# Query-key scores of the sliding-window layer: fp32 products or three float32r products of high and low parts

## The chip, the cores and the metric

One core of a Trainium2 chip runs one program. The metric is device time in microseconds; the kernel before takes 1897.34 us, the median of 3 runs (1896.95 to 1898.87).

## What is computed

A model of three blocks on 512 tokens of width 1024: gated linear attention with an MLP, sliding-window attention with an MLP, and a block with a convolution, dilated attention and a gated MLP. The change touches the attention of the second block. There 16 query heads of width 64 share 2 key heads, in blocks of 128 queries with a band of up to 256 keys:

```python
proj = h @ w_in + b_in
q, k, v = jnp.split(proj, [1024, 1152], axis=-1)
s = jnp.einsum('bnqkgd,bnskd->bnkgqs', q, kb).astype(jnp.float32) * (SWA_HEAD_DIM ** -0.5)
s = jnp.where(valid[None, :, None, None], s, -jnp.inf)
mx = jnp.maximum(jnp.max(s, axis=-1, keepdims=True), sink)
e = jnp.exp(s - mx)
p = e / (jnp.sum(e, axis=-1, keepdims=True) + jnp.exp(sink - mx))
o = jnp.einsum('bnkgqs,bnskd->bnqkgd', p.astype(vb.dtype), vb)
return o.reshape(B, T, 1024) @ w_out + b_out
```

## The kernel before, in words

Each engine has its own program, and the order of the work on an engine is the order in which its function is written. The engines meet through named events: `k.mark` raises one, `k.on` waits for it.

All large matrix products are made in parts. ScalarE rounds a weight tile to float32r (its high part, L1354), VectorE subtracts that from the tile (its low part, L2117), and TensorE adds three float32r products in a PSUM bank: high by high, low by high and high by low (`product`, L553 to L555). A product of an input-projection tile is 8 chunks of these three, 24 matmuls of 128x512.

The sliding-window layer (`t_swa`, `a_swa`, `v_swa`) works on the 8 pairs of heads p = 0 to 7, of which each pair takes one tile of 128 projected query columns: head s of the pair lies on partitions 64s to 64s+63, and both keys lie so in `WK`. The unit `u` is the key tile, `u+1` the value tile, and `u+2+p` the query tile of pair p. The tiles `u` to `u+3` are projected before the loop, in `t_starts`; `u+4` is projected at p = 0, `u+5` at p = 1, and so on to `u+9` at p = 5, all of these in PSUM bank 0. ScalarE brings each finished query tile from PSUM to `WQ`, scaled by 1/8 and with its bias (`evac`, L1674), and marks it with the event `ae`. That event does two things: `score(p)` on TensorE waits for it, and the next product in bank 0 waits for it, since the bank is then free.

In one turn of TensorE's loop stand, from p = 2 on: `score(p)`, `out(p-2)` (probabilities by values, L1112), the first half of the product of `u+4+p`, the transposes of head 2p-2 (L1098), the second half, and the transposes of head 2p-1. At p = 0 the first half of a product stands ahead of the score, and at p = 1 there is no `out` between the score and the product. At p = 6 and 7 pieces of the output projection (`ahead`, L584 to L586) stand where the products were.

`score(p)` is 8 fp32 matmuls of half rows (L1083): four query blocks by two heads, of 128 keys for the first block and 256 for the others. The two heads of a block follow each other and use different rows and different banks. The trace shows each fp32 matmul as two instructions, so 16 for each score.

In one turn of VectorE's loop stand: the masked row maxima of heads 2p and 2p+1 (`score`, L2665), the low part of an attention output (`low`, L2694), the low part of a weight tile (`v_cut`, L2117), the division of head 2p (`weigh`, L2677 to L2683), a copy of transposed probabilities (`turn`, L2690) and the division of head 2p+1. ScalarE has the exponentials (`expo`, L1694, L1696), the query evacuation, the copies of transposed probabilities (L1686) and the high part of the attention output (`high`, L1701):

```python
    for p in range(8):
        score(2 * p)
        score(2 * p + 1)
        if p >= 2:
            low(p - 2)
        v_cut(e, k, u + min(p, 6) + 7)
        weigh(2 * p)
        if p >= 1:
            turn(2 * p - 1)
        weigh(2 * p + 1)
```

Of the kernel before, what the change touches and what calls it, by code (L numbers as in the profile page):

```python
# [8 lines left out]
F32 = mybir.dt.float32  # L9
# [4 lines left out]
T = 512  # L14
# [9 lines left out]
KB = 1024  # L24
# [236 lines left out]
def memory(nc):  # L261
# [77 lines left out]
    m.SVH = over("SVH", [128, 4, 4, 256], rows, F32R)  # L339

    m.WQ = arena("WQ", [128, 8, T], 0)
    m.PW = arena("PW", [128, 4, 896], 16)
    m.PTW = arena("PTW", [128, 2, 896], 30)
    m.WOH = arena("WOH", [128, 8, T], 37, F32R)
# [714 lines left out]
def t_swa(e, k):  # L1059
    m, ps = k.m, k.m.ps  # L1060
    u = k.at["swa_in"]

    def set_v():
        e.wait_ge(*k.on("ae", u + 1))
        e.wait_ge(*k.on(*k.free[7]))
        for t in range(4):
            x = e.transpose(ps[7][:, t * 128:(t + 1) * 128], m.WQ[:, 7, t * 128:(t + 1) * 128], cst(m, "ident"))
        x.then_inc(*k.mark("wvt"))
        k.free[7] = ("wv",)

    def score(p):

        e.wait_ge(*k.on("ae", u + 2 + p))
        e.wait_ge(*k.on("ae", u))
        for g, group in enumerate(SWA_GROUPS):
            f = 0
            for s in range(2):
                e.wait_ge(*k.on(*k.free[SWA_BANKS[g][s]]))
            for blk in group:
                k0, n = SWA_KEYS[blk]  # L1080
                for s in range(2):
                    b, half = SWA_BANKS[g][s], slice(64 * s, 64 * s + 64)
                    x = e.matmul(ps[b][:, f:f + n], m.WQ[half, p, blk * 128:(blk + 1) * 128], m.WK[half, k0:k0 + n],  # L1083
                                 start=True, stop=True)
                    if blk == group[-1]:
                        x.then_inc(*k.mark("score", "w", 2 * p + s, g))
                        k.free[b] = ("smax", "w", 2 * p + s, g)
                f += n

    def turn(i):  # L1090

        for g in range(2):
            b, f = (3, 6)[g], 0
            e.wait_ge(*k.on("pn", "w", i))
            e.wait_ge(*k.on(*k.free[b]))
            for j, blk in SWA_TURNS[g]:
                c = SWA_PLACE[blk] + j * 128 - SWA_KEYS[blk][0]
                x = e.transpose(ps[b][:, f:f + 128], m.PW[:, i % 4, c:c + 128], cst(m, "ident"))  # L1098
                f += 128
            x.then_inc(*k.mark("turn", "w", i, g))  # L1100
            k.free[b] = ("ptv" if i % 2 and g else "pta", "w", i, g)

    def out(p):

        e.wait_ge(*k.on("wv"))
        e.wait_ge(*k.on(*k.free[7]))
        for j, f in ((0, 0), (2, 256), (1, 512), (3, 768)):
            n = min(256, 512 - 128 * j)
            for s in range(2):
                i, half = 2 * p + s, slice(64 * s, 64 * s + 64)  # L1110
                e.wait_ge(*k.on("ptv" if s and j % 2 else "pta", "w", i, j % 2))
                x = e.matmul(ps[7][half, 128 * j:128 * j + n], m.WV[:, j, half], m.PTW[:, s, f:f + n], start=j == 0,  # L1112
                             stop=j == 3, skip_group_check=True)
                if j == 3:
                    x.then_inc(*k.mark("pv", "w", i))
        k.free[7] = ("wol", p)

    t_starts(e, k, u, "mix1", ["ae"] * 4)
    set_v()
    def ahead(c, n, f):  # L1120

        w = k.at["swa_out"]
        tokens(e, k, w + c, n, m.WOH, m.WOL, c, 0, 0, None, lambda c: [("wol", c)], c == 0, False, (f,))

    for p in range(8):
        if p:
            score(p)
        if p >= 2:
            out(p - 2)
        if p < 6:  # L1130
            product(e, k, u + 4 + p, m.HH, m.HL, 2, 0, ev="ae", c1=4)
            if p == 0:
                score(p)
            if p >= 1:
                turn(2 * p - 2)
            product(e, k, u + 4 + p, m.HH, m.HL, 2, 0, ev="ae", c0=4)
            if p >= 1:
                turn(2 * p - 1)
        else:
            if p == 6:  # L1140
                ahead(0, 2, 0)
            turn(2 * p - 2)
            if p == 6:
                ahead(2, 1, 0)
            else:
                ahead(3, 1, 0)
                ahead(0, 2, 1)
            turn(2 * p - 1)
            if p == 7:
                ahead(2, 2, 1)  # L1150

    def between(n):
        if n == 0:
            out(6)
        elif n < 3:
            turn(13 + n)
        else:
            out(7)

    t_ends_early(e, k, k.at["swa_out"], m.WOH, m.WOL, "mlp1", "mv", lambda c: [("wol", c)], between)  # L1160
# [494 lines left out]
def a_swa(e, k):  # L1655
    m, ps = k.m, k.m.ps
    u = k.at["swa_in"]
    bq8 = m.SMALL[:, 56:64]
    e.wait_ge(*k.on("par"))
    e.activation(bq8, par(m, "swa_bq"), AF.Copy, scale=0.125).then_inc(*k.mark("b8", 0))  # L1660
    e.activation(m.SMALL[:, 55:56], par(m, "qn"), AF.Copy, scale=0.125).then_inc(*k.mark("b8", 1))

    def evac(j):
        p = psum(k, u + j)
        e.wait_ge(*k.on("unit", u + j))
        if j == 0:
            e.activation(m.WK[:, :], p, AF.Identity, bias=par(m, "swa_bk")).then_inc(*k.mark("ae", u + j))
        elif j == 1:
            e.activation(m.WQ[:, 7, :], p, AF.Identity, bias=par(m, "swa_bv")).then_inc(*k.mark("ae", u + j))
        else:  # L1670
            e.wait_ge(*k.on("b8", 0))
            if j == 9:
                e.wait_ge(*k.on("wvt"))
            e.activation(m.WQ[:, j - 2, :], p, AF.Identity, bias=bq8[:, j - 2:j - 1], scale=0.125).then_inc(  # L1674
                *k.mark("ae", u + j))

    def set_v():
        e.wait_ge(*k.on("wvt"))
        e.activation(m.WV[:, :, :], ps[7][:, :].rearrange("p (t f) -> p t f", t=4), AF.Copy).then_inc(*k.mark("wv"))

    def turn(i, g):
        a, b = SWA_COLS[g]
        e.wait_ge(*k.on("turn", "w", i, g))
        if i >= 2:
            e.wait_ge(*k.on("pv", "w", i - 2))
        e.activation(m.PTW[:, i % 2, a:b], ps[(3, 6)[g]][:, 0:b - a], AF.Copy).then_inc(*k.mark("pta", "w", i, g))  # L1686

    def expo(i):
        st = m.STAT[:, i % 4, :]
        nm, sm = st[:, 4:8], st[:, 8:12]  # L1690
        e.wait_ge(*k.on("nmax", "w", i))
        for blk in range(4):
            p = m.PW[:, i % 4, SWA_PLACE[blk]:SWA_PLACE[blk] + SWA_KEYS[blk][1]]
            e.activation(p, p, AF.Exp, bias=nm[:, blk:blk + 1], accum_out=sm[:, blk:blk + 1]).then_inc(  # L1694
                *k.mark("exp", "w", i, blk))
        e.activation(st[:, 12:16], nm, AF.Exp, bias=par(m, "sinks", 8 * (i % 2) + i // 2, 1)).then_inc(  # L1696
            *k.mark("exp", "w", i, 4))

    def high(c):
        e.wait_ge(*k.on("pv", "w", 2 * c + 1))  # L1700
        e.activation(m.WOH[:, c, :], ps[7][:, :], AF.Copy).then_inc(*k.mark("woh", c))  # L1701

    for j in range(1, 5):
        a_cut(e, k, u + j + 3)
        evac(j - 1)
    set_v()
    for p in range(8):
        a_cut(e, k, u + min(p, 6) + 7)
        if p == 1:
            turn(0, 0)  # L1710
            turn(0, 1)
        if p < 7:
            expo(2 * p)
        if p >= 2:
            if p != 6:
                high(p - 2)
            turn(2 * p - 2, 0)
            turn(2 * p - 2, 1)
            if p == 6:
                high(p - 2)  # L1720
        if p == 7:
            expo(2 * p)
            turn(2 * p - 1, 0)
        if p == 0:
            evac(p + 4)
        expo(2 * p + 1)
        if 0 < p < 6:
            evac(p + 4)
        if 1 <= p < 7:
            turn(2 * p - 1, 0)  # L1730
    high(6)
    turn(14, 0)
    turn(14, 1)
    turn(15, 0)
    high(7)
    a_ends(e, k, k.at["swa_out"], k.at["up10"], "post_mix1", "mlp1", early=True)
# [914 lines left out]
def v_swa(e, k):  # L2651
# [40 lines left out]
    def low(c):  # L2692
        e.wait_ge(*k.on("woh", c))
        e.tensor_tensor(m.WOL[:, c, :], ps[7][:, :], m.WOH[:, c, :].bitcast(F32), A.subtract).then_inc(*k.mark("wol", c))  # L2694

    for j in range(1, 5):
        v_cut(e, k, u + j + 3)
    for p in range(8):
        score(2 * p)
        score(2 * p + 1)  # L2700
# [4 lines that stand above are left out]
        if p >= 1:  # L2705
            turn(2 * p - 1)
        weigh(2 * p + 1)
    low(6)
    turn(15)
    low(7)  # L2710
# [730 lines left out]
```

## Time and profile before

| what | value |
|---|---|
| median of the runs | 1897.34 us |
| the profiled execution's own time | 1897.22 us |
| its span | 1895.4 us |
| TensorE busy | 1888.0 us of the span |
| VectorE busy | 1344.2 us |
| ScalarE busy | 987.4 us |
| granted TensorE clock | 1.000 |
| sliding-window attention | about 586 to 675 us of the span |

The span runs from the first to the last instruction; the own time of the execution is 1.8 us longer. Shares are means over stages: a wait of TensorE counts fully only where TensorE is the engine that everything else keeps up with.

### The profile page before, as it was taken

The page shows a single profiled execution, that of the slowest core. Times are in us where ns is not written, and L with a number is a line of the kernel's source. Part 1 is how long each engine was busy: PE and PEld are TensorE (multiplying, and loading weights), DVE is VectorE, ACT ScalarE, POOL GpSimd, SP SyncE. Part 2 cuts the span into 40 slices and gives each one's busy share as a digit, 9 for nine tenths or more (in the row PEclk, how much of TensorE's full clock was granted, in tenths as well). Part 3 has the DMA queues.
Part 4 walks back from the last instruction along what each step waited for, and adds up shares of the span by engine and source line. Part 5 has one row for each costly group of instructions (what it writes and reads, how often), then busy time and mean ns, then how long its engine had stood idle before and what let it go on. Part 6 is the DMA issues. An engine that isn't in the chain of part 4 may idle for free. (4 is left out here: it accounts for less than half of the span.)

```text
span 1895.4 us, 25267 instructions
## 1 busy us (share of the span) xinstructions
PE 1888.0 (100%) x9396; PEld 1551.5 (82%) x9396; DVE 1344.2 (71%) x2000; ACT 987.4 (52%) x1591; POOL 96.0 (5%) x114
## 2 busy tenths in 40 slices
PE   9999999999999999999999999999999999999999
PEld 8877888888888788888888888667788888888887
DVE  8656665656566766665666788998897876767867
ACT  5634464444546756454544335788435455545454
POOL 0100000101000000000100000000000000100101
PEclk9999999999999999999999999999999999999999
DMA  6632156757323114756641346232224634644735
GB/s 227 161 100 101 67 152 174 167 164 207 126 69 143 46 66 132 192 145 178 173 160 67 122 134 171 85 95 73 90 95 139 167 93 153 156 150 117 199 96 123
DMA packets 70684, 249.79 MB, mean 132 GB/s; under 512 B 7970, under 2 KB 8226, under 8 KB 69924
## 3 DMA queue, kind: packets, MB, share of 16 engines
q1 hardware_dynamic: 56448, 198.82, 30.4%
q0 software_dynamic: 13824, 49.29, 14.7%
q8 instruction: 77, 1.26, 0.3%
q14 instruction: 43, 0.35, 0.1%
q10 hardware_dynamic: 292, 0.07, 0.0%
HBM read 246.05 MB, written 2.10 MB: 131 GB/s over the span
## 5 line engine op out<-in xcount | busy, mean ns | idle before, releaser
L553 PE MATMUL ps<-HH,WH 128*128 128x512 f32 (+1 forms) x1664 | 620.5, 373 | 0.0
L555 PE MATMUL ps<-HH,WL 128*128 128x512 f32 (+1 forms) x1664 | 615.5, 370 | 0.0
L554 PE MATMUL ps<-HL,WH 128*128 128x512 f32 (+1 forms) x1664 | 615.4, 370 | 0.0
L1354 ACT ACTIVATE WH<-WR 128x1024 fp32r<-128x1024 f32 x331 | 346.8, 1056 | 474.9 <-PE ps L555 311.2
L2117 DVE TENSOR_TENSOR WL<-WR,WH 128x1024 fp32r<-128x1024 f32 x330 | 400.7, 1219 | 262.4 <-ACT WH L1354 262.0
L553 PEld LDWEIGHTS ps<-HH,WH 128*128 128x128 f32 x1664 | 313.5, 188 | 62.8 <-issue 10.0
L555 PEld LDWEIGHTS ps<-HH,WL 128*128 128x128 f32 x1664 | 313.5, 188 | 53.7
L554 PEld LDWEIGHTS ps<-HL,WH 128*128 128x128 f32 x1664 | 313.7, 189 | 52.0
L1012 PE MATMUL ps<-WH,AH 128*128 128x512 f32 x490 | 190.6, 389 | 0.0
L1013 PE MATMUL ps<-WH,AL 128*128 128x512 f32 x490 | 190.6, 389 | 0.0
L1014 PE MATMUL ps<-WL,AH 128*128 128x512 f32 x490 | 190.6, 389 | 0.0
L2726 DVE SCALAR_TENSOR_TENSOR M<-AP,PAR,M 128x512 f32<-128x512 f32 x240 | 167.1, 757 | 0.1
L1013 PEld LDWEIGHTS ps<-WH,AL 128*128 128x128 f32 x490 | 92.0, 188 | 19.2
L1012 PEld LDWEIGHTS ps<-WH,AH 128*128 128x128 f32 x490 | 92.0, 188 | 19.1
L1014 PEld LDWEIGHTS ps<-WL,AH 128*128 128x128 f32 x490 | 92.0, 188 | 19.1
L2006 ACT ACTIVATE UP<-ps 128x512 f32<-128x512 f32 x44 | 26.3, 598 | 117.6 <-PE ps L555 117.6
L3179 POOL DMA_DIRECT2D WR<-in_quart x48 | 41.8, 988 | 813.5 <-DMA WR<-in_quart 745.8
L3040 DVE SCALAR_TENSOR_TENSOR RW<-UP,PAR,RW 128x512 f32<-128x512 f32 x44 | 33.1, 752 | 44.0 <-ACT RW L2012 43.3
L3040 DVE SCALAR_TENSOR_TENSOR M<-UP,PAR,M 128x512 f32<-128x512 f32 x44 | 33.1, 752 | 38.0 <-ACT M L2012 37.3
L1611 ACT ACTIVATE RW<-RW 128x512 f32<-128x512 f32 x64 | 40.5, 632 | 2.0
L1808 ACT ACTIVATE P<-P,SMALL 128x128 f32<-128x128 f32 (+1 forms) x64 | 35.1, 550 | 11.2 <-DVE SMALL L2761 11.2
L1363 ACT ACTIVATE HL<-X 128x1024 fp32r<-128x1024 f32 x22 | 23.3, 1059 | 33.0 <-DVE X L2178 24.7
(401 smaller groups left out, 2614.5 us busy)
## 6 DMA issues: line engine op xcount, KB each, us to landing
WR<-in_up SPq DMA_DIRECT2D x96, 512.0 KB, 4.3
WR<-in_quart SPq DMA_DIRECT2D x60, 512.0 KB, 3.5
WR<-in_quart POOLq DMA_DIRECT2D x48, 512.0 KB, 6.1
WR<-in_in SPq DMA_DIRECT2D x48, 512.0 KB, 3.5
WR<-in_down SPq DMA_DIRECT2D x16, 512.0 KB, 3.4
WR<-in_quartf SPq DMA_DIRECT2D x14, 512.0 KB, 3.5
WR<-in_quartf POOLq DMA_DIRECT2D x14, 512.0 KB, 5.5
MT<-in_up SPq DMA_DIRECT2D x12, 512.0 KB, 3.6
```

What stands on the lines that cost most here:

```text
L553: e.matmul(ps, wh, hi[:, c, cols], start=c == 0 and not (shared and h), stop=False, skip_group_check=shared)
L554: e.matmul(ps, wh, lo[:, c, cols], start=False, stop=False, skip_group_check=shared)
L555: y = e.matmul(ps, wl, hi[:, c, cols], start=False, stop=c == x.n - 1, skip_group_check=shared)
L1012: e.matmul(m.ps[b + v], xh, x.wh[:, w], start=start and q == 0, stop=False, skip_group_check=last)
L1013: e.matmul(m.ps[b + v], xl, x.wh[:, w], start=False, stop=False, skip_group_check=last)
L1014: y = e.matmul(m.ps[b + v], xh, x.wl[:, w], start=False, stop=stop and q == n - 1, skip_group_check=last)
L1354: e.activation(x.wh[:, 0:n], raw(m, x.raw)[:, 0:n], AF.Copy).then_inc(*k.mark("whi", u))
L1611: e.activation(buf, buf, AF.Square).then_inc(*k.mark("sqr", u))
L2117: e.tensor_tensor(x.wl[:, 0:n], raw(m, x.raw)[:, 0:n], x.wh[:, 0:n].bitcast(F32), A.subtract).then_inc(*k.mark("wlo", u))
L2726: e.scalar_tensor_tensor(m.M[:, c, :], m.AP[:, c, t:t + T], par(m, "conv_w", c * 31 + t, 1), m.M[:, c, :], A.mult, A.add).then_inc(*k.mark ...
L3040: e.scalar_tensor_tensor(tmp, m.UP[:, 2 * (i % 2) + g, t:t + T], par(m, "fcw", (i + FC2 * g) * 3 + t, 1), tmp, A.mult, A.add).then_inc(*k. ...
L3179: e.dma_start(raw(m, x.raw)[:, 0:128 * x.n], x.more, accum_op=A.add).then_inc(*k.mark(f"added{x.raw}", u + j, by=16))
```

## The change

The scores are made from parts too. The scale of 1/8 and the key bias go into the key tile `WK`, of which ScalarE makes the high part `WKH` and VectorE the low part `WKL`. ScalarE now writes a query tile from PSUM, with its bias, straight to its high part `WQH`, which has two buffers. A new instruction of VectorE, `low_q(p)`, reads the same PSUM bank, adds the bias, subtracts `WQH` and writes the low part `WQL`; it marks `hlo`. Both `score(p)` and the next product in bank 0 now wait for `hlo` in place of `ae`. Each score is 24 float32r matmuls in place of 8 fp32 ones. `low_q(0)` and `low_q(1)` stand among the weight cuts ahead of VectorE's loop, `low_q(p+2)` is the last thing of turn p, for p = 0 to 5.

```diff
@@ t_swa
     def score(p):
-        e.wait_ge(*k.on("ae", u + 2 + p))
-        e.wait_ge(*k.on("ae", u))
+        e.wait_ge(*k.on("hlo", u + 2 + p))
+        e.wait_ge(*k.on("hlo", "k"))
+        qh, ql = m.WQH[:, p % 2, :], m.WQL[:, p, :]
...
-                for s in range(2):
-                    b, half = SWA_BANKS[g][s], slice(64 * s, 64 * s + 64)
-                    x = e.matmul(ps[b][:, f:f + n], m.WQ[half, p, blk * 128:(blk + 1) * 128], m.WK[half, k0:k0 + n],
-                                 start=True, stop=True)
+                for j, (query, key) in enumerate(((qh, m.WKH), (qh, m.WKL), (ql, m.WKH))):
+                    for s in range(2):
+                        b, half = SWA_BANKS[g][s], slice(64 * s, 64 * s + 64)
+                        x = e.matmul(ps[b][:, f:f + n], query[half, blk * 128:(blk + 1) * 128], key[half, k0:k0 + n],
+                                     start=j == 0, stop=j == 2)
...
-    t_starts(e, k, u, "mix1", ["ae"] * 4)
+    t_starts(e, k, u, "mix1", ["ae", "ae", "hlo", "hlo"])
...
-            product(e, k, u + 4 + p, m.HH, m.HL, 2, 0, ev="ae", c1=4)
+            product(e, k, u + 4 + p, m.HH, m.HL, 2, 0, ev="hlo", c1=4)
...
-            product(e, k, u + 4 + p, m.HH, m.HL, 2, 0, ev="ae", c0=4)
+            product(e, k, u + 4 + p, m.HH, m.HL, 2, 0, ev="hlo", c0=4)
@@ a_swa, evac(j)
         if j == 0:
-            e.activation(m.WK[:, :], p, AF.Identity, bias=par(m, "swa_bk")).then_inc(*k.mark("ae", u + j))
+            e.wait_ge(*k.on("b8", 0))
+            e.activation(m.WK[:, :], p, AF.Identity, bias=bk8, scale=0.125).then_inc(*k.mark("ae", u + j))
+            e.wait_ge(*k.on("ae", u + j))
+            e.activation(m.WKH[:, :], m.WK[:, :], AF.Copy).then_inc(*k.mark("hhi", "k"))
...
-            e.activation(m.WQ[:, j - 2, :], p, AF.Identity, bias=bq8[:, j - 2:j - 1], scale=0.125).then_inc(
-                *k.mark("ae", u + j))
+            if j > 3:
+                e.wait_ge(*k.on("score", "w", 2 * j - 7, 1))
+            e.activation(m.WQH[:, j % 2, :], p, AF.Identity, bias=par(m, "swa_bq", j - 2, 1)).then_inc(*k.mark("ae", u + j))
@@ v_swa
+    def low_q(p):
+        e.wait_ge(*k.on("ae", u + 2 + p))
+        if p == 7:
+            e.wait_ge(*k.on("wvt"))
+        e.scalar_tensor_tensor(m.WQL[:, p, :], psum(k, u + 2 + p), par(m, "swa_bq", p, 1), m.WQH[:, p % 2, :].bitcast(F32),
+                               A.add, A.subtract).then_inc(*k.mark("hlo", u + 2 + p))
+
     for j in range(1, 5):
         v_cut(e, k, u + j + 3)
+        if j == 1:
+            e.wait_ge(*k.on("hhi", "k"))
+            e.tensor_tensor(m.WKL[:, :], m.WK[:, :], m.WKH[:, :].bitcast(F32), A.subtract).then_inc(*k.mark("hlo", "k"))
+        elif j > 2:
+            low_q(j - 3)
...
         weigh(2 * p + 1)
+        if p < 6:
+            low_q(p + 2)
```

TensorE at p = 1, before: the score of the second pair and the start of the next product. `s_ae` is the event of ScalarE's evacuation.

```order
L1083 MATMUL ps<-WK,WQ 128x128 [waits s_smax,s_ae]
L1083 MATMUL ps<-WK,WQ 128x128
L1083 MATMUL ps<-WK,WQ 128x256 x2
L1083 MATMUL ps<-WK,WQ 128x256 [waits s_smax]
L1083 MATMUL ps<-WK,WQ 128x256 x3
L553 MATMUL ps<-HH,WH 128x512 [waits s_ae,s_wlo]
L554 MATMUL ps<-HL,WH 128x512
```

The same place after the change:

```order
L1089 MATMUL ps<-WKH,WQH 128x128 [waits s_smax,s_hlo]
L1089 MATMUL ps<-WKH,WQH 128x128
L1089 MATMUL ps<-WKL,WQH 128x128 x2
L1089 MATMUL ps<-WKH,WQL 128x128 x2
L1089 MATMUL ps<-WKH,WQH 128x256 x2
L1089 MATMUL ps<-WKL,WQH 128x256 x2
L1089 MATMUL ps<-WKH,WQL 128x256 x2
L1089 MATMUL ps<-WKH,WQH 128x256 [waits s_smax]
...
L557 MATMUL ps<-HH,WH 128x512 [waits s_hlo,s_wlo]
```

The score has 24 matmuls in place of 8, and both it and the product behind it wait for VectorE's `s_hlo`.

VectorE at the end of turn p = 0, before: the division of head 1 (`s_exp` is ScalarE's last exponential of a head), then the maxima of head 2.

```order
L2677 TENSOR_TENSOR SMALL<-SMALL 128x4 [waits s_exp]
L2679 RECIPROCAL SMALL<-SMALL 128x4 [waits s_sum]
L2683 TENSOR_SCALAR PW<-PW,SMALL 128x128 [waits s_den]
L2683 TENSOR_SCALAR PW<-PW,SMALL 128x256 [waits s_den] x3
L2665 ISA PW,SMALL<-ps,CONST 128x128 [waits s_par,s_score]
```

The same place after the change:

```order
L2684 TENSOR_TENSOR SMALL<-SMALL 128x4 [waits s_exp]
L2686 RECIPROCAL SMALL<-SMALL 128x4 [waits s_sum]
L2690 TENSOR_SCALAR PW<-PW,SMALL 128x128 [waits s_den]
L2690 TENSOR_SCALAR PW<-PW,SMALL 128x256 [waits s_den] x3
L2707 SCALAR_TENSOR_TENSOR WQL<-ps,PAR,WQH 128x512 [waits s_ae]
L2672 ISA PW,SMALL<-ps,CONST 128x128 [waits s_par,s_score]
```

The low part of the third query tile stands behind the division of head 1, and ahead of the maxima of head 2.

## Rows read from the trace of the kernel before

**Rows 1.** The page, span, busy time and granted clock.

```profile
span 1895.4 us, 25267 instructions
...
PE 1888.0 (100%) x9396; PEld 1551.5 (82%) x9396; DVE 1344.2 (71%) x2000; ACT 987.4 (52%) x1591; POOL 96.0 (5%) x114
...
PEclk9999999999999999999999999999999999999999
```

**Rows 2.** Waits of PE: us in total, times, longest us.

```profile
PE ps L941 <- DVE SMALL L3141: 1.2, 1, 1.2
```

**Rows 3.** Timeline, PE at p = 1: start us, us, engine, line, operation [idle before].

```profile
590.90 1.79 PE L1083 MATMUL ps<-WK,WQ 64*128 64x128 f32 x16
592.62 0.50 PE L553 MATMUL ps<-HH,WH 128*128 128x512 f32 x1
```

**Rows 4.** Timeline, ACT and DVE between 588 and 596 us.

```profile
588.04 0.43 DVE L2665 CUSTOM_DVE_ANT_0 PW<-ps,CONST 128x256 f32<-128x256 f32 x1 [0.22 <-PE ps L1083]
...
591.19 0.67 ACT L1674 ACTIVATE WQ<-ps,SMALL 128x512 f32<-128x512 f32 x1
...
593.62 0.29 ACT L1696 ACTIVATE SMALL<-SMALL,PAR 128x4 f32<-128x4 f32 x1
...
...
595.34 0.28 DVE L2665 CUSTOM_DVE_ANT_0 PW<-ps,CONST 128x128 f32<-128x128 f32 x1
```

**Rows 5.** Groups by line and form: count, busy us, mean ns of one.

```profile
L2319 DVE SCALAR_TENSOR_TENSOR LA<-ps,LA 128x512 f32<-128x512 f32 x4 | 2.5, 684 | 2.1 <-ACT LA L1471 2.1
L2743 DVE SCALAR_TENSOR_TENSOR QK<-QK,PAR,AT 128x512 f32<-128x512 f32 x8 | 6.0, 745 | 0.0
```

**Rows 6.** Timeline: one pair of score instructions, and whole-row float32r matmuls of 256 columns.

```profile
592.31 0.38 PE L1083 MATMUL ps<-WK,WQ 64*128 64x256 f32 x2
...
568.57 0.28 PE L554 MATMUL ps<-HL,WH 128*128 128x256 f32 x1
568.69 0.28 PE L555 MATMUL ps<-HH,WL 128*128 128x256 f32 x1
```

**Rows 7.** Timeline, PE and its weight loads (PEld) around `out(0)`, p = 2.

```profile
601.61 2.42 PE L1112 MATMUL ps<-PTW,WV 128*64 128x256 f32 x16
...
602.30 1.49 PEld L1112 LDWEIGHTS ps<-PTW,WV 128*64 128x64 f32 x14 [0.50 <-ACT PTW L1686]
```

**Rows 8.** Timeline, one whole turn, p = 3, from 611 us.

```profile
611.29 0.56 DVE L2690 COPY PTW<-ps 128x384 f32<-128x384 f32 x1 [1.04 <-PE ps L1098]
...
613.15 0.28 DVE L2665 CUSTOM_DVE_ANT_0 PW<-ps,CONST 128x128 f32<-128x128 f32 x1
...
614.56 0.50 PE L553 MATMUL ps<-HH,WH 128*128 128x512 f32 x1
...
618.07 0.98 ACT L1686 ACTIVATE PTW<-ps 128x512 f32<-128x512 f32 x2 [0.65 <-PE ps L1098]
```

**Rows 9.** Timeline, DVE and ACT, from the end of p = 5 to p = 7.

```profile
643.21 0.56 DVE L2690 COPY PTW<-ps 128x384 f32<-128x384 f32 x1 [1.25 <-PE ps L1098]
...
645.07 0.28 DVE L2665 CUSTOM_DVE_ANT_0 PW<-ps,CONST 128x128 f32<-128x128 f32 x1
...
646.70 0.40 ACT L1694 ACTIVATE PW<-PW,SMALL 128x128 f32<-128x128 f32 x1 [2.14 <-DVE SMALL L2671]
...
650.22 0.69 DVE L2694 TENSOR_TENSOR WOL<-ps,WOH 128x512 fp32r<-128x512 f32 x1 [2.05 <-ACT WOH L1701]
650.83 1.22 DVE L2117 TENSOR_TENSOR WL<-WR,WH 128x1024 fp32r<-128x1024 f32 x1
...
653.36 0.55 DVE L2690 COPY PTW<-ps 128x384 f32<-128x384 f32 x1
```

**Rows 10.** Timeline, PE: `out(4)`, `out(5)` and `out(6)`.

```profile
644.82 1.73 PE L1112 MATMUL ps<-PTW,WV 128*64 128x256 f32 x16
...
652.09 2.74 PE L1112 MATMUL ps<-PTW,WV 128*64 128x256 f32 x16
...
659.88 2.02 PE L1112 MATMUL ps<-PTW,WV 128*64 128x256 f32 x16
```

More of the change, by code:

```diff
@@ L341, in memory @@
     m.WQ = arena("WQ", [128, 8, T], 0)
+    m.WQL = arena("WQL", [128, 8, T], 0, F32R)
+    m.WKL = over("WKL", [128, T], acc, F32R)
+    m.WKH = over("WKH", [128, T], dg + 2 * KB, F32R)
+    m.WQH = over("WQH", [128, 2, T], tmp, F32R)
     m.PW = arena("PW", [128, 4, 896], 16)
@@ L1080, in score @@
                 k0, n = SWA_KEYS[blk]
-                for s in range(2):
-                    b, half = SWA_BANKS[g][s], slice(64 * s, 64 * s + 64)
-                    x = e.matmul(ps[b][:, f:f + n], m.WQ[half, p, blk * 128:(blk + 1) * 128], m.WK[half, k0:k0 + n],
-                                 start=True, stop=True)
-                    if blk == group[-1]:
-                        x.then_inc(*k.mark("score", "w", 2 * p + s, g))
-                        k.free[b] = ("smax", "w", 2 * p + s, g)
+                for j, (query, key) in enumerate(((qh, m.WKH), (qh, m.WKL), (ql, m.WKH))):
[3 more added lines that the diff above has]
+                                     start=j == 0, stop=j == 2)
+                        if blk == group[-1] and j == 2:
+                            x.then_inc(*k.mark("score", "w", 2 * p + s, g))
+                            k.free[b] = ("smax", "w", 2 * p + s, g)
                 f += n
@@ L1657, in a_swa @@
     u = k.at["swa_in"]
-    bq8 = m.SMALL[:, 56:64]
+    bk8 = m.SMALL[:, 56:57]
     e.wait_ge(*k.on("par"))
-    e.activation(bq8, par(m, "swa_bq"), AF.Copy, scale=0.125).then_inc(*k.mark("b8", 0))
+    e.activation(bk8, par(m, "swa_bk"), AF.Copy, scale=0.125).then_inc(*k.mark("b8", 0))
     e.activation(m.SMALL[:, 55:56], par(m, "qn"), AF.Copy, scale=0.125).then_inc(*k.mark("b8", 1))
@@ L1670, in evac @@
         else:
-            e.wait_ge(*k.on("b8", 0))
-            if j == 9:
-                e.wait_ge(*k.on("wvt"))
-            e.activation(m.WQ[:, j - 2, :], p, AF.Identity, bias=bq8[:, j - 2:j - 1], scale=0.125).then_inc(
-                *k.mark("ae", u + j))
+            if j > 3:
+                e.wait_ge(*k.on("score", "w", 2 * j - 7, 1))
+            e.activation(m.WQH[:, j % 2, :], p, AF.Identity, bias=par(m, "swa_bq", j - 2, 1)).then_inc(*k.mark("ae", u + j))
     def set_v():
```

## Prediction

> **What bounds the kernel now.** I read the page first. TensorE is busy for 1888.0 us of a span of 1895.4 us, at the full granted clock (2.4 GHz) throughout [rows 1], and the waits of TensorE name none longer than 1.2 us [rows 2]. So the kernel is bound by what TensorE has to do, and a change counts in two ways only: by how much shorter its instructions get, and by waits that it puts into a row of instructions that has none. The other engines have time to spare, VectorE 551 us, but only where nobody waits for the place at which their new work stands. After the page I read the timeline of the attention turn by turn, for that.
>
> **The scores themselves.** One score starts at 590.90 and the next product at 592.62: 1.72 us [rows 3]. It is 16 instructions of 0.38 us each; they fit because the two heads start together, on different rows [rows 6]. So a score is 8 pairs, six of 256 columns and two of 128. An fp32 instruction takes each column twice: six pairs of 512 cycles and two of 256 are 3584 cycles, at 2.4 GHz 1.49 us; the other 0.23 us are the start and the change to the next kind of matmul.
>
> After the change a score is 12 pairs of float32r: nine of 256 columns, three of 128. The trace has no float32r matmul on half rows. The nearest row is the float32r matmul on whole rows with 256 columns: they follow each other by 0.12 us [rows 6]. If a pair costs what one whole-row matmul costs, and 128 columns no less than 256 (a load of weights stands ahead of each either way), a score takes 12 x 0.12 + 0.23 = 1.67 us, which **saves 0.05 us**. The bounds: if the pairs run at the bare stream rate, (9 x 256 + 3 x 128) / 2.4 GHz = 1.12 us, plus 0.23, the score saves 0.37 us; if the two heads do not overlap, 24 x 0.12 + 0.23 = 3.11 us, it costs 1.39 us more. I take 0.05, the value of the nearest row with the overlap that the fp32 pairs show.
>
> **The new wait at p = 1.** This is the main term. The product of `u+5` stands right behind `score(1)` and goes into bank 0. Before, the bank was free once ScalarE had evacuated `u+4`, from 591.19 to 591.86 [rows 4], so the product started at 592.62 without waiting. Now it must wait for `low_q(2)`, and that stands on VectorE behind both divisions of turn 0. The division of head 1 waits for the last exponential of head 1, which ends at 593.91; the next thing on VectorE started at 595.34 [rows 4]. That is where `low_q(2)` starts, less the 0.05 us by which `score(0)` is shorter: the second group of maxima did wait for that score [rows 4], and everything behind hangs on it. So it starts at 595.29. The price of `low_q` is that of a scalar_tensor_tensor of 128x512 from PSUM, 0.684 us [rows 5]; the same from SBUF with a parameter column takes 0.745 us [rows 5], the upper bound. It ends at 595.97, and with 0.05 us to hand over (as from ScalarE's copy to the loads at 602.30 [rows 7], whose copy ended at 602.25) the product starts at 596.02. **The cost is 596.02 - 592.62 = 3.40 us**, and what both scores save is already inside it. Behind the product wait the transposes, `score(2)` and all the rest of TensorE's list. VectorE and ScalarE don't get ahead by it for long: ScalarE's copies and exponentials of turn 1 stand behind the transposes of head 0, which stand behind this product, so they move by the same 3.40 us.
>
> **p = 2.** `out(0)` started at 601.61 but had to wait for ScalarE's copy until 602.30 [rows 7]. That chain moves with the transposes and not with the score, so the score's gain is lost here: **0**. `low_q(3)` ends some 0.5 us before the product needs the bank.
>
> **p = 3, 4, 5.** In turn 3 VectorE's copy starts at 611.29, released by TensorE, and the division of head 5 is over when the maxima begin at 613.15; `low_q(4)` would then run from 613.15 to 613.84, and the product starts at 614.56 [rows 8]. So there are 0.7 us of slack and no wait. `low_q` pushes everything behind it on VectorE back by 0.61 us (an instruction of 0.69 us is followed after 0.61 [rows 9]): the maxima, through them the exponentials, the high part and the copy of ScalarE that starts at 618.07 with 0.65 us of idle time ahead of it [rows 8]. It just fits. VectorE too gets to its next copy with 1.04 us to spare [rows 8]. So each of these turns gains the score's 0.05: **-0.15 us**.
>
> **p = 6 and 7.** Here the cover is gone. From the copy at 643.21, released by TensorE's transposes of head 9, VectorE and ScalarE hand over to each other without TensorE: division, [`low_q(7)`], maxima of head 12, exponentials (ScalarE idle until 646.70), high part, low part at 650.22, weight cut, division, and the copy at 653.36 [rows 9], for which `out(5)` waits: it takes 2.74 us in place of the 1.73 of `out(4)`, which waits for nothing [rows 10]. `low_q(7)` stands in this chain, so `out(5)` ends 0.61 us later, and the gains of scores 6 and 7 are lost in it. The same chain goes on to `out(6)`, which also waits (2.02 us [rows 10]); it is the same delay, not a second one. **+0.61 us**.
>
> **What costs nothing.** The extra copy of the keys on ScalarE, `WKL` and the first two `low_q` fall into time in which both engines wait for TensorE's first four products, 0.7 us each against idle times of several us. If `low_q(1)` were late it would hold the second half of `score(0)`; by the end of the weight cut ahead of it, it has about 0.7 us to spare. `low_q` and ScalarE's evacuation read the same bank one after the other.
>
> **Sum.** 3.40 + 0 - 0.15 + 0.61 = **+3.86 us**, on the profiled execution's own 1897.22 us; that execution lies 0.12 us under the median of 1897.34, so against the median I say 1901.2 us. What a measurement of this kernel can tell from no change is about 0.2%, 3.8 us: the sum falls right on this bound.
>
> **Rivals.** *The heads do not overlap* (each score +1.39 us). The wait at p = 1 grows to 3.40 + 0.05 + 1.39 = 4.84, since the chain hangs on `score(0)`; p = 2 hides 0.69 of it (+0.70); three turns 4.17; and at p = 6 the score ends at 644.82 [rows 10] + 1.39 while VectorE would be ready at 645.07 [rows 9] + 0.61: 0.53 on top of 0.61. Sum 10.85, 1908.2 us. For it: no such matmul is in the trace. Against: the fp32 pairs overlap, and with weight loads of the same width.
>
> *Loads don't overlap within a row group.* In this kernel a load for head 0 would then stand behind head 0's running matmul; a pair would take its 256 columns, 0.107 us, and then a load, at most 0.12 since a load and a matmul fit into that on whole rows [rows 6]: 12 x 0.227 + 0.23 = 2.95, +1.23 per score. By the same places: 4.68 + 0.54 + 3.69 + 0.98 = 9.89, 1907.2 us. Against it speak the whole-row matmuls, which reload the same rows each time and still follow by 0.12 [rows 6]. The Trainium skill (TensorE: Matmul & The Clock Gate, "The mechanism") says that weight loads overlap running matmuls only when the row group differs; by that rule this rival would be the forecast. The trace does not agree: 0.12 us for 256 columns leaves no room for a load of its own.
>
> *The clock falls in the wait.* TensorE stands still for about 3.4 us at p = 1, far longer than any wait of the trace before [rows 2], in which the clock never fell [rows 1]. If it fell to 1.2 GHz for the 12 matmuls behind the wait, which take 2.8 us, they would take 2.8 us more: 1904.0 us. The Trainium skill (TensorE: Matmul & The Clock Gate, "Part 1: The HAM clock gate") says the clock is halved after an idle stretch; no row of before can show it.
>
> *The wait is given back*, the case on the other side. TensorE waits later for `out(0)` 0.69, `out(5)` 1.01 and `out(6)` 0.29 us; if the engines behind got ahead during the 3.40 us, these 1.99 us would vanish, the 0.61 with them, and scores at the bare stream rate would save 0.37 in five turns, 1.85: 3.40 - 1.99 - 1.85 = -0.44, 1896.9 us. It decides from a gain of 3.4 us on. Against: the chains to these waits begin at transposes that stand behind the wait.
>
> **Chances.** The forecast 0.68, of which a little over half lies over the bound (0.36 slower, 0.32 same, as scores at the stream rate would bring it down by 1.0); no overlap 0.04 and loads apart 0.04, slower; the clock 0.12, slower; given back 0.07, same; the rest 0.05, 0.03 faster and 0.02 same. That makes faster 0.03, same 0.41, slower 0.56. The range from 1899.3 to 1905.5 holds the forecast with its bounds and the clock, 0.80: below, scores at the stream rate (five turns and the chain, 6 x 0.32 = 1.9), above, the clock with another 1.5 for score or VectorE prices at their upper ends.
>
> **What would show it.** In the profile after: one idle stretch of TensorE of 3.3 to 3.5 us ahead of the product at about 592.5 us, released by VectorE's `WQL`; scores of 24 matmuls in 1.6 to 1.7 us, begun in pairs; `out(5)` longer by 0.3 to 0.7 us; no other new wait. Scores of over 2 us, or no idle stretch at p = 1, would make it wrong.

## The result, and the profile after

The changed kernel takes **1902.85 us** (median of 8 runs, 1902.32 to 1904.29), against 1897.32 us for the kernel before (8 runs, measured together with it): a ratio of 1.003, 95% interval 1.0021 to 1.0039. It is 5.5 us slower. The profiled execution is the first of the runs, 1902.32 us. Its page, the lines that answer to [rows 1]:

```profile
span 1900.5 us, 25405 instructions
...
PE 1888.4 (99%) x9460; PEld 1553.6 (82%) x9460; DVE 1350.2 (71%) x2009; ACT 988.7 (52%) x1592; POOL 96.2 (5%) x114
...
PEclk9999999999999999999999999999999999999999
```

The span is 5.1 us longer, while TensorE's busy time is only 0.4 us longer. So most of it is idle time of TensorE. A slower clock does not show as idle time, and shorter scores can hide it in the sum of the busy time, so it has to be looked for by itself. The waits of PE (us in total, times, longest) name the first; it answers to [rows 2]:

```profile
PE ps L557 <- DVE WQL L2707: 3.7, 1, 3.7
PE ps L945 <- DVE SMALL L3162: 1.2, 1, 1.2
PE ps L1104 <- ACT PTW L1693: 0.6, 1, 0.6
```

There is one wait of 3.7 us, of the product (L557, was L553) for the low part of a query tile. The second row was there before; the third is new. The timeline at p = 1, where [rows 3] and [rows 4] were read (start us, us, engine, line, operation, in brackets the idle time before):

```profile
590.34 0.33 PE L1089 MATMUL ps<-WKH,WQH 64*128 64x128 f32 x2
...
590.65 0.67 ACT L1682 ACTIVATE WQH<-ps,PAR 128x512 fp32r<-128x512 f32 x1
...
593.81 1.07 DVE L2690 TENSOR_SCALAR PW<-PW,SMALL 128x128 f32<-128x128 f32 x4
594.79 0.75 DVE L2707 SCALAR_TENSOR_TENSOR WQL<-ps,PAR,WQH 128x512 fp32r<-128x512 f32 x1
...
595.69 0.47 PE L557 MATMUL ps<-HH,WH 128*128 128x512 f32 x1 [3.67 <-DVE WQL L2707]
```

The tile was ready for `low_q(2)` at 591.32, when ScalarE's evacuation ended. It ran at 594.79, behind both divisions, for 0.75 us; the product started 0.15 us later. The next stretch is what the page does not show, since its 40 slices are too coarse: the windows of TensorE (stretch, length, busy time with the number of instructions, granted clock with 1.00 for 2.4 GHz, DMA share, GB/s).

```profile
593.00:595.50 2.50, 0.00 (x0) 1.00 0.00 0
595.50:596.70 1.20, 1.01 (x4) 0.96 0.00 0
596.90:600.10 3.20, 3.20 (x10) 0.51 0.00 0
600.20:603.60 3.40, 3.40 (x20) 1.00 0.47 159
```

After the wait the clock is full for the first matmuls, then half (1.2 GHz) for 8 of them, then full again. The timeline there:

```profile
595.99 0.40 PE L558 MATMUL ps<-HL,WH 128*128 128x512 f32 x1
596.23 0.39 PE L559 MATMUL ps<-HH,WL 128*128 128x512 f32 x1
...
598.02 0.63 PE L558 MATMUL ps<-HL,WH 128*128 128x512 f32 x1
598.45 0.63 PE L559 MATMUL ps<-HH,WL 128*128 128x512 f32 x1
```

They follow each other by 0.23 to 0.24 us first (0.30 behind the very first), and by 0.43 in the slow stretch. These are busy times, so no list of waits holds them.

**Where the time went.** One place can be compared between all runs without the small differences elsewhere: from the start of `score(0)` to the first transposes of the next layer, on TensorE. Before, that is 586.22 to 693.57; after, 585.79 to 698.54:

```profile
693.57 0.60 PE L608 MATMUL ps<-CONST,MT 128*128 128x128 f32 x4
```

```profile
698.54 0.93 PE L612 MATMUL ps<-CONST,MT 128*128 128x128 f32 x7
```

| stretch on TensorE, us | before | after | difference |
|---|---|---|---|
| `score(0)` to the product of p = 1 | 6.40 | 9.89 | +3.49 |
| that product's start to the transposes of head 0 | 2.87 | 4.41 | +1.54 |
| on to `out(4)` at p = 6 | 49.32 | 48.91 | -0.41 |
| on to the end of the layer | 48.75 | 49.53 | +0.78 |
| together | 107.34 | 112.75 | +5.41 |

What lies outside this stretch took 1788.1 us before and 1787.8 after; over all profiled executions of this study it ranges from 1787.4 to 1789.1, and of that part the kernels change only a few instructions ahead of `score(0)`. So differences of under 1 us are read from the stretch, with the medians beside them.

### The profile page after: what moved, and what is told of

The parts are those of the page before. It is cut to its first block and busy times, and to the rows that moved or that the text cites. A ratio compares the mean times of both kernels' runs of the same rounds, so it can differ in the third digit from the quotient of the medians.

```text
span 1900.5 us, 25405 instructions
## 1 busy us (share of the span) xinstructions
PE 1888.4 (99%) x9460; PEld 1553.6 (82%) x9460; DVE 1350.2 (71%) x2009; ACT 988.7 (52%) x1592; POOL 96.2 (5%) x114
## 5 line engine op out<-in xcount | busy, mean ns | idle before, releaser
L557 PE MATMUL ps<-HH,WH 128*128 128x512 f32 (+1 forms) x1664 | 621.1, 373 | 3.7 <-DVE WQL L2707 3.7
L557 PEld LDWEIGHTS ps<-HH,WH 128*128 128x128 f32 x1664 | 313.8, 189 | 66.4 <-issue 13.2
```

What stands on the lines that cost most here:

```text
L557: e.matmul(ps, wh, hi[:, c, cols], start=c == 0 and not (shared and h), stop=False, skip_group_check=shared)
```

## The experiments

### The clock by itself

The first four kernels (`e1_fill` to `e4_fp32`) were measured together, and the kernel before took 1897.11 us there (27 runs). The first fills the wait with work:

```diff
+FILL = 14
...
+        if p == 1:
+            e.wait_ge(*k.on("wv"))
+            for _ in range(FILL):
+                x = e.matmul(ps[7][:, :], m.HH[:, 0, 0:128], m.HH[:, 1, :], start=True, stop=True)
+            x.then_inc(*k.mark("fill"))
+            k.free[7] = ("fill",)
```

> The changed kernel with 14 more float32r matmuls of 128x512 behind score(1), into PSUM bank 7, whose result nothing reads: they fill the wait for low_q(2), which itself stays. Theory (the time is the wait of 3.5 us, plus the clock at half rate behind it, 1.5 us): TensorE never stands still for long, the granted clock stays at 1.00, and the kernel takes 1.5 us less than the changed one, about 1901.3 us. Rival (the slow matmuls behind the wait have another cause, such as a refill after a wait or contention with VectorE): the matmuls behind the wait stay slow and the time stays at 1902.8, or more.

Measured: 1901.1 us (1900.6 to 1902.47, 11 runs), 1.75 under the changed kernel, or 1.54 when each is taken against its own kernel before (3.99 over 1897.11, 5.53 over 1897.32); the stretch is 111.17, 1.58 shorter. The timeline at p = 1 and two of the same windows:

```profile
591.91 3.47 PE L1138 MATMUL ps<-HH 128*128 128x512 f32 x14
595.66 0.47 PE L558 MATMUL ps<-HH,WH 128*128 128x512 f32 x1 [0.28 <-DVE WQL L2714]
```

```profile
595.50:596.70 1.20, 1.04 (x5) 1.00 0.00 0
596.90:600.10 3.20, 3.20 (x19) 1.00 0.02 5
```

The product starts at 595.66, as late as in the changed kernel, since it waits for the same instruction. But the clock stays at 1.00, and the 3.2 us that held 10 matmuls now hold 19. More work on TensorE made the kernel faster: the slow matmuls came from the idle stretch, and their price is the 1.54 us of the table.

### The wait by itself

The second gives the product of p = 0 another bank, so that the product of p = 1 does not have to wait for `low_q(2)`. The value transposes take bank 0 for it.

```diff
@@ t_swa
-            x = e.transpose(ps[7][:, t * 128:(t + 1) * 128], m.WQ[:, 7, t * 128:(t + 1) * 128], cst(m, "ident"))
+            x = e.transpose(ps[0][:, t * 128:(t + 1) * 128], m.WQ[:, 7, t * 128:(t + 1) * 128], cst(m, "ident"))
...
-        k.free[7] = ("wv",)
+        k.free[0] = ("wv",)
...
-            product(e, k, u + 4 + p, m.HH, m.HL, 2, 0, ev="hlo", c1=4)
+            product(e, k, u + 4 + p, m.HH, m.HL, 2, 0 if p else 7, ev="hlo", c1=4)
...
```

> The changed kernel with one thing moved: the value transposes use bank 0 in place of 7, and the product of p = 0 uses bank 7 in place of 0, so the product of p = 1 waits for an evacuation that is long over and not for low_q(2). All instructions of the change stay. Theory (bank 0 is what couples TensorE to the tail of VectorE's turn): no idle stretch at p = 1, no fall of the clock, scores of 1.6 us; left are the 0.7 us of p = 6 and 7 less 0.1 us for each score that is not hidden (five of them): 1897.3 plus 0.1, about 1897.4 us. Rival (VectorE is too full, and the wait comes back at p = 2 or at the scores): 1900 us or more.

Measured: 1898.0 us (1897.8 to 1898.37, 11 runs), ratio to before 1.0004 (0.9995 to 1.0013); the stretch is 108.28. Wait and fall of the clock are gone, and with them 4.47 us of the 5.41 in the stretch. But it is 0.6 us above the expectation, and the list of waits says where:

```profile
PE ps L1118 <- ACT PTW L1693: 1.1, 2, 1.0
PE ps L1104 <- ACT PTW L1693: 0.6, 1, 0.6
```

`out(0)` (L1118) now waits 1.0 us for ScalarE's copy. I come back to it with `e6_q2`.

### The scores by themselves

```diff
-        e.wait_ge(*k.on("hlo", u + 2 + p))
+        e.wait_ge(*k.on("ae", u + 2 + p))
-        qh, ql = m.WQH[:, p % 2, :], m.WQL[:, p, :]
+        qh, ql = m.WQH[:, p % 2, :], m.WQH[:, p % 2, :]
...
-        if p < 6:
-            low_q(p + 2)
```

> The changed kernel without any low_q: the low part of the queries is not computed, the third product of a score takes the high part again, so its row of 24 float32r matmuls stays; score and product wait for ScalarE's evacuation as before the change. Theory (float32r scores save 0.11 us each, but only where nothing else is waited for: p = 0, 1, 3, 4, 5; low_q costs everything else): 1897.3 - 0.55 = 1896.8 us, no wait at p = 1, and out(5) and out(6) end as before. Rival (the float32r scores cost in another place, or save in all eight turns): over 1897.3, or 1896.4.

Measured: 1896.63 us (1896.17 to 1897.33, 11 runs), ratio 0.9997 (0.9988 to 1.0006); the stretch is 106.96, 0.38 less than before. This kernel leaves out the low part of the queries, so its scores are less exact; only its time is of use. The direction and the mechanism agree. The size is somewhat under the expected 0.55, and the interval of the runs holds no change as well. From `out(4)` on it takes 48.91 us, against 48.75 before and 49.53 after the change: without any `low_q` most of the loss at the end is gone. That is the third term by subtraction, 0.6 us.

### The scores as before, with the wait

```diff
-                for j, (query, key) in enumerate(((qh, m.WKH), (qh, m.WKL), (ql, m.WKH))):
+                for j, (query, key) in enumerate(((q32, m.WK),)):
```

> The changed kernel with the scores as before: 8 fp32 matmuls each, on the unsplit keys (the low part of the keys is not made) and on the rounded queries; low_q and all waits for it stay, and its result is not used. Theory (wait, clock and the chain at p = 6 cost 5.7 us, the shorter scores give 0.4 back): 0.4 us slower than the changed kernel, about 1903.2 us, with the same idle stretch at p = 1, 0.1 longer. Rival (the scores' new form is what costs): near 1897.3.

Measured: 1904.08 us (1903.0 to 1905.53, 5 runs), ratio 1.0037 (1.0024 to 1.0049); the stretch is 113.02, 0.27 over the changed kernel. Its product of p = 1 starts 10.01 us behind `score(0)`, 0.12 more. The rival, that the new form of the scores costs, is out: with the old form the loss is as large. The medians differ by 1.2 us, three times the expected 0.4, and more than the stretch; 0.6 of it lies outside the stretch in the profiled execution, and with 5 runs the cause of that stays open.

The clock fell here too. The idle stretch ahead of the product is 3.54 us (596.40), the granted clock is 0.50 from there on, and from 596.96 the matmuls follow each other by 0.42 to 0.43 us up to 599.09, then by 0.23 again. From the product to the transposes of head 0 it takes 4.23 us, against 2.87 before the change and 4.41 after it. So the fall is seen behind two idle stretches of this length, at a price of 1.36 and 1.54 us.

### The place of one instruction

The kernels `e5_first` to `e8_q2q7r` were measured together (before: 1897.15 us, 33 runs), and `e9_mid` to `e11_best` likewise (before: 1897.33 us, 27 runs). `e5_first` leaves the banks of the change and moves `low_q(2)`:

```diff
         v_cut(e, k, u + min(p, 6) + 7)
+        if p == 0:
+            low_q(2)
         weigh(2 * p)
...
-        if p < 6:
+        if 0 < p < 6:
             low_q(p + 2)
```

> The changed kernel with low_q(2) moved on VectorE from behind both divisions of turn 0 to ahead of them; banks as in the change. Theory (the position of one instruction makes the wait, and a short wait leaves the clock alone): low_q(2) runs as soon as ScalarE's evacuation is over (591.9), the wait shrinks from 3.7 to about 0.7 us, the granted clock stays at 1.00, maxima and exponentials of turn 1 come no later: 1897.1 + 0.7 + 0.7 (chain at p = 6) - 0.55 = about 1898.0 us. Rival (any wait at this place drops the clock): 1899.5 or more.

Measured: 1897.55 us (1896.99 to 1898.6, 11 runs), ratio 1.0 (0.9992 to 1.0009); the stretch is 107.75, so 5.00 us of 5.41 are back. The wait is even shorter than expected:

```profile
591.58 0.75 DVE L2707 SCALAR_TENSOR_TENSOR WQL<-ps,PAR,WQH 128x512 fp32r<-128x512 f32 x1 [1.30 <-ACT WQH L1682]
...
592.47 0.47 PE L557 MATMUL ps<-HH,WH 128*128 128x512 f32 x1 [0.23 <-DVE WQL L2707]
```

VectorE had been idle for 1.30 us when `low_q(2)` could start. Between this kernel and the changed one lies the place of one instruction, and nearly the whole loss.

A wait between the two comes from the third possible place, behind the first division:

```diff
         weigh(2 * p)
+        if p == 0:
+            low_q(2)
...
-        if p < 6:
+        if 0 < p < 6:
             low_q(p + 2)
```

> The changed kernel with low_q(2) between the two divisions of turn 0. By the timeline of VectorE the first division ends at about 592.7, low_q(2) at 593.4: a wait of 1.5 us ahead of the product of p = 1, between the 0.2 of e5_first and the 3.7 of the change. Theory (a wait costs its length, and the clock falls only behind the long one): clock 1.00 throughout, 1.3 us more than e5_first, about 1898.8 us. Rival (the clock falls behind this one too): about 1900.3 us.

Measured: 1898.88 us (1898.06 to 1900.14, 11 runs), ratio 1.0008 (0.9999 to 1.0017). Its waits of PE and its cores:

```profile
PE ps L557 <- DVE WQL L2707: 1.0, 1, 1.0
```

```profile
core 0: 1897.1 us, clock 1.000
```

The clock stays full behind this wait. The stretch is 108.52, 0.77 over e5_first; I had expected 1.3. `low_q(2)` ended at 593.16 where I had put it at 593.4, and the score ended at 592.25 and not at 591.9. So a wait of 1.0 us costs its length alone, and only those of 3.5 and 3.7 us cost 1.4 to 1.5 more. No run has a wait between 1.0 and 3.5 us.

### The wait of `out(0)`

```diff
         score(2 * p)
+        if p in (1,):
+            low_q(p + 1)
         score(2 * p + 1)
...
-        if p < 6:
+        if 0 < p < 6:
             low_q(p + 2)
```

> The kernel with the swapped banks (e2_bank), low_q(2) moved once more: between the maxima of head 2 and head 3. In e2_bank out(0) waited 1.0 us for ScalarE's copy, 0.8 more than before: my theory is that low_q(2) ahead of the maxima delays the exponentials of head 2 and with them that copy. Then here out(0) waits as before the change and the kernel takes 0.7 us less than e2_bank, 1897.3. Rival (the copy is late because TensorE came 0.7 us earlier to it): no gain, 1898.0.

Measured: 1897.56 us (1897.17 to 1898.44, 11 runs), ratio 1.0001 (0.9993 to 1.001); the stretch is 107.87, 0.41 under e2_bank. First e2_bank, then this kernel: when VectorE finished the maxima of head 2 (L2678), and how `out(0)` went on behind ScalarE's copy.

```profile
596.77 0.23 DVE L2678 TENSOR_SCALAR SMALL<-SMALL,PAR 128x4 f32<-128x4 f32 x1
...
602.36 1.73 PE L1118 MATMUL ps<-PTW,WV 128*64 128x256 f32 x14 [0.97 <-ACT PTW L1693]
```

```profile
596.19 0.23 DVE L2678 TENSOR_SCALAR SMALL<-SMALL,PAR 128x4 f32<-128x4 f32 x1
...
601.88 1.73 PE L1118 MATMUL ps<-PTW,WV 128*64 128x256 f32 x14 [0.41 <-ACT PTW L1693]
```

Both explanations hold in part. Moved, `low_q(2)` no longer delays the maxima, and `out(0)` waits 0.41 in place of 0.97. What is left is that TensorE gets there earlier: counted from the start of `score(0)`, `out(0)` goes on with its weight loads behind the copy after 16.05 us here (601.88) and after 16.08 before the change (602.30 in [rows 7]), so the copy is as early as it was.

### The end of the layer

```diff
@@ e7_q2q7 against e6_q2: v_swa
         score(2 * p)
-        if p in (1,):
+        if p in (1, 6):
             low_q(p + 1)
...
-        if 0 < p < 6:
+        if 0 < p < 5:
             low_q(p + 2)
@@ e8_q2q7r: also t_swa, p = 6
-            if p == 6:
-                ahead(0, 2, 0)
             turn(2 * p - 2)
             if p == 6:
+                ahead(0, 2, 0)
                 ahead(2, 1, 0)
```

> As e6_q2, and low_q(7) too between the maxima of heads 12 and 13, so that it leaves the chain of p = 6 that ends in the wait of turn(11) and out(5); the pieces of the output projection at p = 6 then wait for it, about 0.8 us, where TensorE has about 1 us to spare before out(5). Theory: 0.4 to 0.7 us less than e6_q2, about 1896.8. Rival (the new wait is handed on whole): the same as e6_q2 or 0.2 more.

> As e7_q2q7, and on TensorE at p = 6 the transposes of head 10 stand ahead of the first piece of the output projection, so that nothing waits for low_q(7). Theory: the chain is as before the change and all of the scores' gains that are left outside waits stay, 1896.6, 0.5 under the kernel before. Rival: the transposes then wait for a bank, no better than e7_q2q7.

Measured: e7 1897.73 us (1897.24 to 1898.23, 11 runs), e8 1897.01 us (1896.3 to 1897.86, 11 runs); ratios 1.0001 (0.9993 to 1.001) and 0.9998 (0.9989 to 1.0007). The stretches are 108.08 and 107.24. From `out(4)` to the end it is 49.52 us in e6, 49.74 in e7, 48.88 in e8 and 48.75 before the change. My expectation of `e7_q2q7` fell, and its rival holds: the delay is handed on whole. In e7 the output projection's first piece (L588) is late by 1.0 us, the longest of these two waits:

```profile
PE ps L588 <- issue: 1.4, 2, 1.0
```

The list names no engine for it. But the piece uses bank 0, which `low_q(7)` frees, and that ended at 646.41, 0.07 us ahead of the weight load of this piece (646.48). This pushes back the transposes of head 10, and they are themselves a link of the chain to `out(5)`, through ScalarE's copy. e8 takes them out of the way, and then the end of the layer costs 0.13 us more than before the change in place of 0.78. So the chain is what I took it for, but it has a link on TensorE that I had left out. No run has the new order on TensorE without the move of `low_q(7)`, so how much of the 0.65 us the order alone would give, in this kernel or in the one before, stays open.

### How much room there is in the middle turns

```diff
         if 0 < p < 6:
             low_q(p + 2)
+            if p < 5:
+                e.wait_ge(*k.on("hlo", u + 4 + p))
+                low_q(p + 2)
```

> e5_first with low_q done twice in turns 1 to 4, the second behind the first: 0.8 us more on VectorE per turn, with no use. The prediction called low_q free in these turns, with 0.7 us of room ahead of the product and 0.65 us on ScalarE. Theory (it is free, and the room is nearly used up): each of four products now waits about 0.3 us, 1.2 us in all, about 1898.8 us. Rival (there is much more room): 1897.6 us as e5_first.

Measured: 1898.56 us (1898.23 to 1900.64, 11 runs), ratio to before 1.0008 (0.9999 to 1.0017); the stretch is 109.00, 1.25 over e5_first. All of it lies between the first transposes and `out(4)`: 50.22 us in place of 48.92.

```profile
PE ps L557 <- DVE WQL L2707: 1.5, 5, 0.3
```

Five products wait, for 0.3 us each at most. One of the five is that of p = 1, with the 0.2 of e5_first; the four others are those of the doubled instructions. One `low_q` per turn is hidden, a second is not: it adds 0.78 us to VectorE's turn, and 0.3 of that reaches TensorE. So there was room for about 0.5 us more, and not for 0.7. In the changed kernel `low_q(4)` ended at 618.51, 0.54 us ahead of the product at 619.05, and the hand-over takes 0.14 of that.

### Both moves together

`low_q(2)` ahead of the divisions as in e5_first, the end as in e8_q2q7r, the banks of the change.

> The two moves that paid, together, with the banks of the change: low_q(2) ahead of both divisions of turn 0 (e5_first), low_q(7) between the maxima of heads 12 and 13 and the transposes of head 10 ahead of the first piece of the output projection (e8_q2q7r). Theory (all that is left is 0.11 us for each score outside a wait): over the stretch from score(0) to the end of the layer 0.4 us less than before the change, 1896.8 us, which the runs can hardly tell from 1897.15. Rival (the two moves don't add, since the wait of out(0) is there in both): 1897.2 us.

Measured: 1896.75 us (1896.23 to 1898.01, 11 runs); ratio 0.9998 (0.9989 to 1.0007). The stretch is 107.09, 0.25 less than before the change. The moves add: 5.66 us against the changed kernel in the stretch, where the first gave 5.00 (`e5_first`) and the second 0.63 (`e8_q2q7r` against `e6_q2`). Against the kernel before no gain can be told from none.

## Why the prediction was right, and where it was off

The time of 1902.85 us lies in the range of 1899.3 to 1905.5, and it is slower, as the larger chance said. The forecast of 1901.2 was 1.6 us low. The steps:

- **The new wait at p = 1**: 3.40 predicted, 3.49 measured. The mechanism is shown by moving one instruction (`e5_first`) and by taking away the shared bank (`e2_bank`). Three parts of it were off, and two of them nearly cancel. `low_q(2)` started 9.00 us behind `score(0)`, where I had 9.07: 0.07 less, from the shorter score. It took 0.06 longer. And the product started 0.15 us behind its end, where I had taken 0.05 from the hand-over of ScalarE's copy to a weight load [rows 7]: 0.10 more. For the price of `low_q` I took 0.684 us from the PSUM row of [rows 5]; the trace after has eight of them:

```profile
L2707 DVE SCALAR_TENSOR_TENSOR WQL<-ps,PAR,WQH x8: 746/747/748, 579.5 to 649.4; 128x512 fp32r<-128x512 f32 x8
```

The median is 0.747 us, which is the other row of [rows 5], named as the upper bound. The row at 0.684 us has the constant 0.0 as its scalar and the others a parameter column, which is the one difference that I can name (the output type is not it, as the row at 0.745 us writes float32 too); no run here tests it.

- **The clock falls in the wait**: this was a rival with 0.12, and it is what the forecast lacked. It fell, for +1.54 us, and 3.86 + 1.54 is 5.40, against the 5.41 of the table. That the sum meets so well is luck: by the rows of the table the forecast was 0.09 us too low for the wait, 0.26 too high for the middle turns and 0.17 too low for the end, and these cancel. My price for it was 2.8 us, for 12 slow matmuls; 8 were slow, as the clock was still full for those right behind the wait, and full again at the transposes. The step that failed is the chance. The trace of before had no idle stretch longer than 1.2 us [rows 2] and so could not speak for or against it, while the Trainium skill (TensorE: Matmul & The Clock Gate, "Part 1: The HAM clock gate") gives a half clock after an idle stretch as a rule. This trace agrees with the rule: 0.51 in the window behind 3.67 us of idle time, 1.00 in the same window with the idle time filled (`e1_fill`), 0.50 behind 3.54 us (`e4_fp32`) and 1.00 behind 1.05 us (`e9_mid`). It deserved to be the likelier case.

- **The scores themselves**: 0.05 us each predicted, 0.11 measured. Score and step to the next kind of matmul took 1.72 us, and now take 587.40 - 585.79 = 1.61:

```profile
585.79 0.33 PE L1089 MATMUL ps<-WKH,WQH 64*128 64x128 f32 x2
585.96 0.28 PE L1089 MATMUL ps<-WKL,WQH 64*128 64x128 f32 x2
...
587.07 0.28 PE L1089 MATMUL ps<-WKL,WQH 64*128 64x256 f32 x2
587.19 0.28 PE L1089 MATMUL ps<-WKH,WQL 64*128 64x256 f32 x2
587.40 0.50 PE L557 MATMUL ps<-HH,WH 128*128 128x512 f32 x1
```

The pairs are pairs, and they follow each other by 0.12 us at 256 columns, and at 128 by hardly less, 0.11. That is as taken from [rows 6], and both rivals on the overlap are out. The term of 0.23 us for the ends was too large: 1.61 is 12 x 0.12 and 0.17. From the last pair to the product it is 0.21 us now, where the last fp32 pair started 0.31 ahead of it (592.31 in [rows 6], 592.62 in [rows 3]). But a pair takes 0.12 now and took 0.22 then (the fp32 pairs start at 591.66, 591.88, 592.10 and 592.31), so the step to the next kind of matmul costs 0.09 us over a pair in both kernels.

- **p = 2 gains nothing**: right. TensorE is 4.48 us behind the kernel before at the start of `out(0)` and 4.61 at its end, so the score's gain is lost there. The experiment with the banks (`e2_bank`) showed more: this wait is the next in line if the first is removed.

- **p = 3, 4, 5**: -0.15 predicted, -0.41 measured up to `out(4)`, which has four scores in it of 0.11 each. That `low_q` is hidden in these turns, and only just, is shown by `e10_double`.

- **p = 6 and 7**: +0.61 predicted from the end of p = 5, with the gain of score 6 lost in it. From the transposes of head 9 the delay goes from 4.31 to 4.97 us, +0.66; from `out(4)` on it is +0.78. The chain, in the timeline after (it answers to [rows 9] and [rows 10]):

```profile
649.38 0.75 DVE L2707 SCALAR_TENSOR_TENSOR WQL<-ps,PAR,WQH 128x512 fp32r<-128x512 f32 x1
...
651.67 0.40 ACT L1701 ACTIVATE PW<-PW,SMALL 128x128 f32<-128x128 f32 x1 [2.80 <-DVE SMALL L2678]
...
653.74 0.95 ACT L1693 ACTIVATE PTW<-ps 128x512 f32<-128x512 f32 x2
...
654.46 0.96 PE L1104 MATMUL ps<-CONST,PW 128*128 128x128 f32 x7 [0.64 <-ACT PTW L1693]
```

ScalarE was idle for 2.80 us ahead of the exponentials, 2.14 before [rows 9]. The delay reached TensorE one place earlier than I said: at the transposes of head 11, which wait for their bank, and `out(5)` merely passed it on.

- **The wait is given back**, the rival on the other side: it was not. Behind the wait the difference stays at 4.6 us from the first transposes to p = 3, since the other engines' work hangs on those transposes.

- **What would show it**: the scores of 1.61 us lie where I said. The idle stretch of 3.67 us lies above the 3.3 to 3.5 that I gave as a sign. `out(5)` is longer by 0.14 us (2.88 against 2.74) and not by 0.3 to 0.7, and there is one other new wait, of 0.6 us, at the transposes of head 11: the delay at the end came as large as forecast, but at another place.

The effect of 5.5 us is 1.4 times the forecast of 3.9, and the 1.6 us between them is the clock, at 1.54.

## What to carry to other kernels

When an instruction is added whose end frees a buffer, look first at where it stands in its own engine's order, not at its price: `low_q(2)` costs 0.75 us, and behind two divisions it held up TensorE for 3.5. Put it where its input becomes ready, and check every turn of a loop by itself, as the first and the last lack the work that gives the cover in the middle. And price an idle stretch of TensorE of several us above its length: here the clock behind 3.7 us of it added another 1.5, while behind 1.0 us it added nothing.

## What was not expected of the hardware

- Filling an idle stretch of TensorE with 14 useless matmuls made the kernel 1.54 us faster (each against its own kernel before), though the product behind the wait started as late as without them.
- Float32r matmuls on half rows overlap in pairs like fp32 ones, and a pair of 128 columns takes 0.11 us where one of 256 takes 0.12. Three products of parts on half rows save only 0.11 us of 1.72 against the fp32 form, though by the prediction's count of columns they would take 1.12 us in place of 1.49.
- The step from a score to the next product costs 0.09 us over the last pair, whether the score is in fp32 (0.31 against 0.22) or in float32r (0.21 against 0.12).
